# Softmax steps of VectorE taken in pairs, and three changes of sequence in the two layers, in a two-block transformer kernel

## The chip, the cores and the metric

The kernel runs on one core of one Trainium2 chip. The metric is the device time of one execution in microseconds (us). PE is TensorE, DVE is VectorE, ACT is ScalarE, POOL is GpSimd, SP is SyncE, which here only issues the transfers of weights.

## What is computed

256 tokens of width 1024 pass through two blocks, all in f32. Cut to what matters here:

```
# first block
h = rms_norm(x, g) * (1 + scale1) + shift1;  q, k, v, u, z = split(h @ w_in)      # 8 heads of 64
s = q @ k.T * 64**-0.5 + bias;  s = where(key <= query, s, -1e30);  p = softmax(s);  a = p @ v
mixed = (sigmoid(z1) * (a @ w_a) + sigmoid(z2) * (pool(u) @ w_p)) @ w_out;  x = x + gate1 * mixed
x = x + gate2 * moe(rms_norm(x) ...)       # 32 experts, the two best of a token
x = rms_norm(x, norm_f_g)
# second block, two layers
h = rms_norm(x);  a_q, a_i, a_zf, a_zb, a_g, b_u, c_q, c_k, c_v = split(h @ w_in)
o_a = hgrn2(a_q, a_i, a_zf, a_zb, a_g)     # gated scan, both directions
o_b = real(fft2(b_u))                      # over tokens and the channels of a group
o_c = attention(rotary(c_q), rotary(c_k), c_v)   # three dilated windows, here one softmax with a mask term, 8 heads
x = x + concat(o_a, o_b, o_c) @ w_out
x = x + square(relu(rms_norm(x) @ w_up)) @ w_down
```

## The kernel before

Every engine has a program of its own, written out in its final order (`pe_...`, `act_...`, `dve_...`). Nothing is rescheduled: an engine runs its list from top to bottom and stops at a semaphore until it is reached. PE writes into eight PSUM banks of 512 columns. `g.take` gives out the next bank of a rota and makes PE wait until the reader of the bank's previous content is done. `g.full` is the reader's wait for PE, and `g.evac` PE's wait for a reader. Weights come in tiles of 1 MB through a ring of SBUF slots that SP refills in the order of use.

**First block, attention.** `pe_first` does eight tiles of the gate projection (L541, two chunks `("gate", n)` each). After each tile comes a step of attention, `pe_attention_step(c)`: the scores of two heads (`pe_scores`, L566; two blocks of queries each, 128 keys for the first, 256 for the second), the turning of the probabilities of the step before (`pe_turn`, L575) and the product with v of the step before that (`pe_mix`, L589). DVE does for each of the four score tiles of a step in `dve_scores`: scale and add the bias (L1635), row maximum (L1638), wait for ACT's exponential with its row sum (ACT, L1272), reciprocal (L1640), multiplication (L1642). Between two steps DVE accumulates a product with the conditioning vector (`dve_ada`, L1650 and L1653) and later adds a bias to what PE makes of it (`dve_ada_bias`, L1661), which frees the PSUM bank of PE's L634. ACT does the exponentials, then copies the turned probabilities (L1279), then the gates (L1342), each time with a reload of its function table.

**The layers** (`pe_layer`, twice). PE alternates between projections (L541, L553) and the small products of the three mixers. `pe_hgrn` makes the far products (L1125, L1131) and seven levels of near ones (L1146); ACT copies the far products in `act_far` (L1566, L1567). `act_turn_halves` issues four transfers from ACT's queue (L1527), which swap the halves of c_q or c_k for the rotation. `pe_hgrn_out` (L1171, L1173) waits for ACT's last copies of the pair sums (L1456). Then come the first stage of the Fourier mixer (L989, four products), a product of ones (L993), and the attention in four steps of two heads. One step is S, scores (L1186); T, turning (L1199); M, the product with v (L1212). Between them lie four pieces O of the output projection, `pe_out_first` (L1231), which need none of the attention. In the text S1 is the scores of heads 2 and 3, S2 those of heads 4 and 5, S3 those of heads 6 and 7; T1, M1 and O1 likewise, and each counts from 0.

DVE's side of the layers' attention is a list in a fixed order:

```python
    for h in range(2, 8):
        dve_layer_score(e, g, l, h)
        if h > 2:
            dve_layer_prob(e, g, l, h - 1)
    dve_layer_prob(e, g, l, 7)
```

`dve_layer_score` reads the scores from PSUM (L2218) and takes the maximum (L2220); `dve_layer_prob` is the reciprocal (L2226) and two multiplications (L2230). T of a head waits in `pe_layer_turn` for that head's `dve_layer_prob`, by `e.wait_ge(g.s["prob_ready"], 8 * l + h + 1)`.

Of the kernel before, what the change touches and what calls it, by code (L numbers as in the profile page):

```python
# [8 lines left out]
AX = mybir.AxisListType  # L9

P = 128
D = 1024
S = 256
KC = D // P
ST = S // P
HEADS, DH = 8, 64
# [927 lines left out]
def pe_layer(e, g, l):  # L944
    s = g.s
    n = 2 + 2 * l
    ready = lambda k: h_ready(e, g, n, k)
    raw = lambda which: lambda k: e.wait_ge(s["xw"], KC * (2 * l + which) + k + 1)

    def project(tile, oc):  # L950
        w = g.filled(e, layer_tile(l, tile))
        for jj in range(2):
            pe_chunk(e, g, ("in", l, oc + jj), w, jj, 256, KC, g.h, ready)
        g.owed += 1

    def tokens(tile, j):
        w = g.filled(e, layer_tile(l, tile))
        pe_tokens(e, g, ("av", l, j), w, g.h, ready)
        g.owed += 1

    for tile in range(2):
        w = g.filled(e, layer_tile(l, tile))
        for jj in range(2):
            pe_chunk(e, g, ("in", l, 4 + 2 * tile + jj), w, jj, 256, KC, g.xw, raw(0))
            if tile == jj == 0 and l:
                pe_norm_added(e, g, n)
            if tile == 0 and jj == 1 and l == 0:
                pe_norm_two(e, g)
        g.owed += 1
    project(2, 0)  # L970
    tokens(3, 0)
    project(4, 10)
    project(5, 12)
    pe_hgrn(e, g, l, 0, 0)
    pe_hgrn(e, g, l, 0, 1)
    project(6, 14)
    project(7, 16)
    project(8, 2)
    pe_hgrn(e, g, l, 1, 0)
    project(9, 8)  # L980
    pe_hgrn(e, g, l, 1, 1)
    tokens(10, 1)
    pe_hgrn_out(e, g, l)
    for c in range(2):
        for tt in range(ST):
            u = g.take(e, ("V", l, c, tt))
            e.wait_ge(s["late_in"], 16)
            g.evac(e, "in", l, 8 + c)
            g.last(u, e.matmul(u.ap[:, 0:S], g.uT[:, c, tt * P:(tt + 1) * P], g.c("dft_c"), start=True, stop=True))  # L989
    u = g.take(e, ("os", l))  # L990
    e.wait_ge(s["o_square"], 2 * l + 2)
    for c in range(2):
        ins = e.matmul(u.ap[:, c * S:(c + 1) * S], g.c("headones"), g.tmp4[:, c, :], start=True, stop=True)  # L993
    g.last(u, ins)
    pe_layer_scores(e, g, l, 0)
    tokens(11, 2)
    for c in range(2):
        u = g.take(e, ("four", l, c))
        e.wait_ge(s["late_in"], 16)
        for tt in range(ST):  # L1000
            g.evac(e, "V", l, c, tt)
        for n4 in range(4):
            part, tt = n4 // 2, n4 % 2
            ins = e.matmul(u.ap[:, 0:S], g.V[:, tt, c, part * P:(part + 1) * P], g.c("dft_t", (part * ST + tt) * S, S), start=n4 == 0, stop=n4 == 3)
        g.last(u, ins)

    g.cycle, g.turn = range(4), 0
    out = []
    pe_layer_scores(e, g, l, 1)
    pe_layer_turn(e, g, l, 0)  # L1010
    pe_layer_scores(e, g, l, 2)
    pe_out_first(e, g, l, out)
    pe_layer_turn(e, g, l, 1)
    pe_layer_mix(e, g, l, 0)
    pe_layer_scores(e, g, l, 3)
    pe_out_first(e, g, l, out)
    pe_layer_turn(e, g, l, 2)
    pe_layer_mix(e, g, l, 1)
    pe_out_first(e, g, l, out)
    pe_layer_turn(e, g, l, 3)  # L1020
    pe_layer_mix(e, g, l, 2)
    pe_out_first(e, g, l, out)
    pe_layer_mix(e, g, l, 3)
    g.cycle, g.turn = range(8), 0
    for j in range(4):
        w = g.filled(e, layer_tile(l, 12 + j))
        for jj in range(2):
            for k in range(4, KC):
                g.evac(e, "m", l, k - 4)
                ins = e.matmul(out[j].ap[:, jj * S:(jj + 1) * S], w[:, k * 256 + jj * P:k * 256 + (jj + 1) * P], g.mix[:, k, :],  # L1030
                               start=False, stop=k == KC - 1, skip_group_check=True)
                if k < KC - 1:
                    g.hand_back(ins)
        g.last(out[j], ins)
        g.owed += 1

    for j in range(2):
        w = g.filled(e, layer_tile(l, 16 + j))
        for jj in range(2):
            oc = 2 * j + jj  # L1040
            pe_chunk(e, g, ("up", l, oc), w, jj, 256, KC, g.xw, raw(1))
            if oc == 0:
                pe_norm_added(e, g, n + 1)
        g.owed += 1
    for i in range(SEVENS):
        pe_seven(e, g, l, i)
    w = g.filled(e, layer_tile(l, 18 + SEVENS))
    e.wait_ge(s["hid_ready"], UPS * (l + 1))
    for jj in range(2):
        pe_chunk(e, g, ("down", l, jj), w, jj, 256, KC, g.hid[:, 24:32, :], lambda k: None)  # L1050
    g.owed += 1
# [102 lines left out]
def pe_hgrn_out(e, g, l):  # L1154
    for dr in range(2):
        for j in range(2):
            g.evac(e, "far", l, dr, j)
    e.wait_ge(g.s["far_out"], 4 * (l + 1))
    e.wait_ge(g.s["placed"], 2 * (l + 1))
    g.evac(e, "av", l, 0, 1)  # L1160
    for c in range(2):
        u = g.take(e, ("o", l, c))
        for tt in range(ST):
            for far in range(2):
                for j in range(2):
                    lo, hd = DH * j, 2 * c + j
                    v = slice(hd * DH, (hd + 1) * DH)
                    q = u.ap[lo:lo + DH, tt * P:(tt + 1) * P]
                    if far:
                        al = 4 * (1 - tt) + 2 * j + c  # L1170
                        ins = e.matmul(q, g.av[:, 1 - tt, v], g.AL[:, al * P:(al + 1) * P], start=False, stop=True)  # L1171
                    else:
                        ins = e.matmul(q, g.av[:, tt, v], g.AT[:, hd, tt * P:(tt + 1) * P], start=True, stop=False)  # L1173
                    if tt == far == 1 and j == 0:
                        ins.then_inc(g.s["o_half"], 1)
        g.last(u, ins)


def pe_layer_scores(e, g, l, c):

    us = [g.take(e, ("s", l, 2 * c + j)) for j in range(2)]
    e.wait_ge(g.s["rot_ready"], 4 * l + 3 + c // 2)
    for qt in range(ST):
        for j in range(2):
            lo = DH * j
            ins = e.matmul(us[j].ap[:, qt * S:(qt + 1) * S], g.cq[lo:lo + DH, c, qt * P:(qt + 1) * P], g.ck[lo:lo + DH, c, :],  # L1186
                           start=True, stop=True)
            if qt == 1:
                g.last(us[j], ins)


def pe_layer_turn(e, g, l, c):
    for j in range(2):
        h = 2 * c + j
        u = g.take(e, ("t", l, h))
        e.wait_ge(g.s["prob_ready"], 8 * l + h + 1)
        for kt in range(ST):
            for qt in range(ST):
                ins = e.transpose(u.ap[:, (2 * kt + qt) * P:(2 * kt + qt + 1) * P], g.prob[h % 4][:, qt * S + kt * P:qt * S + (kt + 1) * P],  # L1199
                                  g.c("ident"))  # L1200
        g.last(u, ins)
# [192 lines left out]
def act_layer(e, g, l):  # L1394
    s = g.s
# [40 lines left out]
            tokens(0)  # L1436
    for oc in range(10, 14):
        evict(oc)
    act_turn_halves(e, g, l, 0)
    act_far(e, g, l, 0)  # L1440
    for lv in range(NL):
        act_decay(e, g, l, 1, lv)
        if lv % 2 == 0:
# [15 lines left out]
    for c in range(2):  # L1459
        ps = g.full(e, "o", l, c)[:, 0:S]  # L1460
# [13 lines left out]
    for c in range(2):  # L1474
        ps = g.full(e, "four", l, c)[:, 0:S]
# [145 lines left out]


def dve_scores(e, g, A, c):
    for j in range(2):
        for qt in range(ST):
            s = 4 * c + 2 * j + qt
            nk, hd = A.keys(qt), 2 * c + j
            pr = A.pbuf[s % 8][:, 0:nk]
            m, total = g.small[:, 2 * s:2 * s + 1], g.small[:, 2 * s + 1:2 * s + 2]
            if s == 0:  # L1630
                A.first_score(e)
            if s >= 8:
                g.full(e, A.name, "t", c - 2, j)
            ps = g.full(e, A.name, "s", c, j, qt)
            g.read((A.name, "s", c, j, qt), e.scalar_tensor_tensor(out=pr, in0=ps[:, 0:nk], scalar=DH ** -0.5, in1=A.add(hd, qt),  # L1635
                                                                   op0=ALU.mult, op1=ALU.add))
            g.evac(e, A.name, "s", c, j, qt)
            e.tensor_reduce(m, pr, AX.X, ALU.max, negate=True).then_inc(g.s["row_max"], 1)  # L1638
            e.wait_ge(g.s["row_exp"], A.base + s + 1)
            g.step.up(e.reciprocal(total, total))  # L1640
            g.after(e)
            e.tensor_scalar(pr, pr, total, None, ALU.mult).then_inc(g.s["prob"], 1)  # L1642


def dve_ada(e, g, n):
# [809 lines left out]
```

## Time and profile before

| | |
|---|---|
| time, median of 3 runs | 1407.7 us (1407.31 to 1408.53) |
| time of the profiled execution | 1408.37 us |
| its span in the trace | 1406.6 us |
| mean granted clock of TensorE | 0.996 of full speed |
| PE busy | 1380.7 us, 98% |
| PE weight loads busy | 1061.7 us, 75% |
| DVE busy | 661.8 us, 47% |
| ACT busy | 264.2 us, 19% |
| POOL busy | 4.0 us |

The span is what the profiler sees; the time has 1.8 us more around it. The stages follow each other: first block without experts to about 235 us, experts to about 698 us, first layer to about 1047 us, second layer to the end. A busy PE includes the modelled end of each matmul, some 0.1 us after the next one has begun, so that a short pause between matmuls is a little longer than the idle time that the profile gives it.

### The profile page before, as it was taken

What the parts mean: (1) busy time and instruction counts of PE and PEld (TensorE: products, weight loads), DVE (VectorE), ACT (ScalarE), POOL (GpSimd) and SP (SyncE); (2) the same over time, 40 slices, a digit from 0 to 9 for tenths busy, and PEclk for the clock granted to TensorE, in tenths of its full rate; (3) what the DMA queues carried; (4) which work ended last, traced back from release to release, by engine and by line L of the source; (5) the groups of instructions that cost most, each with busy time, mean ns of one, the idle gap of its engine ahead of it and who ended that gap; (6) DMA issues with size and microseconds to landing.
All of it is one profiled execution on the core that took longest, in us unless ns stands there. A gap on an engine that the chain in (4) does not pass through costs nothing.

```text
span 1406.6 us, 22243 instructions
## 1 busy us (share of the span) xinstructions
PE 1380.7 (98%) x9402; PEld 1061.7 (75%) x9402; DVE 661.8 (47%) x1483; ACT 264.2 (19%) x565; POOL 4.0 (0%) x10
## 2 busy tenths in 40 slices
PE   9999999999999999999999999999999999999997
PEld 6888887454445544554488789999998878999997
DVE  2467554111111111111278837775445883777544
ACT  2234201100000000000243431220014343122000
POOL 0000000000000000000000000000000000000000
PEclk9999999999999999999999999999999999999999
DMA  9995656999999999999944224444544413444420
GB/s 392 354 398 197 265 215 274 422 422 420 420 420 422 420 421 420 423 421 421 418 166 132 83 101 171 178 161 169 181 150 150 151 61 124 171 158 179 165 76 31
DMA packets 51237, 362.95 MB, mean 258 GB/s; under 512 B 6064, under 2 KB 6384, under 8 KB 7872
## 3 DMA queue, kind: packets, MB, share of 16 engines
q1 hardware_dynamic: 48528, 353.39, 63.4%
q10 hardware_dynamic: 2032, 5.96, 1.4%
q0 software_dynamic: 576, 2.14, 0.4%
q8 instruction: 77, 1.26, 0.4%
q14 instruction: 24, 0.20, 0.0%
HBM read 358.31 MB, written 1.06 MB: 255 GB/s over the span
## 4 chain that ended last, share of the span: by engine, by line
PE 92%; DMA 2%; DVE 2%; ACT 1%; issue 1%; ACTq 0%; DVEq 0%; SPq 0%
PE bank L1094 26%; PE bank L839 22%; PE bank L541 19%; PE bank L553 4%; PE bank L827 4%; PE bank L849 4%; DMA ring<-in_weights 2%; PE bank L1231 2%; PE bank L658 2%; PE bank L1030 2%; PE bank L1186 1%; PE bank L1212 1%; PE bank L613 1%; PE bank L1146 1%; PE bank L1199 1%
## 5 line engine op out<-in xcount | busy, mean ns | idle before, releaser
L541 PE MATMUL bank<-h,ring 128*128 128x256 f32 x832 | 185.6, 383 | 0.8 <-issue 0.7
L541 PEld LDWEIGHTS bank<-h,ring 128*128 128x128 f32 x832 | 158.0, 191 | 23.8 <-issue 2.3
L839 PE MATMUL bank<-ring,x_s 128*64 128x512 f32 x768 | 167.8, 592 | 1.4 <-issue 0.9
L839 PEld LDWEIGHTS bank<-ring,x_s 128*64 128x64 f32 x768 | 56.1, 137 | 109.9 <-issue 109.9
L1094 PE MATMUL bank<-hid,ring 128*128 128x128 f32 x912 | 115.6, 275 | 0.0
L1094 PE MATMUL bank<-h,ring 128*128 128x128 f32 x896 | 113.8, 275 | 0.0
L1094 PEld LDWEIGHTS bank<-hid,ring 128*128 128x128 f32 x912 | 108.6, 192 | 0.0
L1094 PEld LDWEIGHTS bank<-h,ring 128*128 128x128 f32 x896 | 107.0, 192 | 0.1
L1936 DVE TENSOR_TENSOR act<-act,bank 128x512 f32<-128x512 f32 x16 | 11.0, 688 | 195.5 <-PE bank L839 195.5
L1094 PE MATMUL bank<-sq,ring 128*128 128x128 f32 x720 | 95.1, 275 | 0.0
L1094 PEld LDWEIGHTS bank<-sq,ring 128*128 128x128 f32 x720 | 87.6, 192 | 0.0
L839 PE MATMUL bank<-ring,a_s 128*64 128x512 f32 x384 | 85.0, 595 | 0.0
L553 PE MATMUL bank<-ring,h 128*128 128x256 f32 x320 | 71.2, 381 | 0.0
L1094 PE MATMUL bank<-ring 128*128 128x128 f32 x512 | 67.6, 275 | 0.0
L553 PEld LDWEIGHTS bank<-ring,h 128*128 128x128 f32 x320 | 60.2, 190 | 9.3 <-issue 1.3
L1919 DVE TENSOR_TENSOR x_s<-bank,mod 128x512 f32<-128x512 f32 x32 | 22.1, 692 | 95.7 <-PE bank L827 95.7
L839 PEld LDWEIGHTS bank<-ring,a_s 128*64 128x64 f32 x384 | 26.5, 137 | 49.4 <-issue 48.0
L1094 PEld LDWEIGHTS bank<-ring 128*128 128x128 f32 x512 | 62.3, 192 | 0.0
L849 PEld LDWEIGHTS bank<-put,gy 128*128 128x128 f32 x256 | 47.3, 190 | 19.8 <-issue 14.0
L827 PE MATMUL bank<-pick,h 128*128 128x128 f32 x512 | 61.4, 279 | 0.7 <-DVE pick L1911 0.7
L827 PEld LDWEIGHTS bank<-pick,h 128*128 128x128 f32 x512 | 59.9, 196 | 0.8 <-issue 0.8
L849 PE MATMUL bank<-put,gy 128*128 128x256 f32 x256 | 59.5, 385 | 1.0 <-DVE gy L1943 1.0
(353 smaller groups left out, 1734.7 us busy)
## 6 DMA issues: line engine op xcount, KB each, us to landing
ring<-in_weights SPq DMA_DIRECT2D x288, 1024.0 KB, 12.4
ringx<-in_weights SPq DMA_DIRECT2D x48, 1024.0 KB, 19.6
x<-in_x SPq DMA_DIRECT2D x1, 1024.0 KB, 5.1
pool_a<-in_cst ACTq DMA_DIRECT2D x1, 1024.0 KB, 6.2
bias<-bias_rows POOLq DMA_DIRECT2D x1, 1024.0 KB, 16.9
ring<-cq ACTq DMA_DIRECT2D x8, 128.0 KB
ring<-ck ACTq DMA_DIRECT2D x8, 128.0 KB, 2.4
out<-h ACTq DMA_DIRECT2D x2, 512.0 KB, 3.6
```

The lines of the kernel that those rows point to most:

```text
L541: ins = e.matmul(u.ap[:, 0:S], w[:, k * width + j * P:k * width + (j + 1) * P], acts[:, k, :], start=k == 0, stop=k == kc - 1)
L553: ins = e.matmul(u.ap[:, 0:256], acts[:, k, tt * P:(tt + 1) * P], w[:, k * 256:(k + 1) * 256], start=k == 0, stop=k == KC - 1)
L613: ins = e.matmul(u.ap[32 * q:32 * q + 32, 0:256], g.spread[:, k, :], w[:, k * 256:(k + 1) * 256], start=m == 0, stop=m == 1)
L658: ins = e.matmul(u.ap[:, 0:S], w[:, k * 256 + jj * P:k * 256 + (jj + 1) * P], g.h[:, k, :], start=k == 0, stop=k == KC - 1)
L827: ins = e.matmul(g.bank[bank + k // 4][:, (k % 4) * P:(k % 4 + 1) * P], g.h_tok[:, tt, k * P:(k + 1) * P], g.pick[:, tt * P:(tt + 1) * P], ...
L839: ins = e.matmul(g.bank[bank][ex * SLOTS:(ex + 1) * SLOTS, :], stat(m)[:, ex * SLOTS:(ex + 1) * SLOTS], pair[ex][:, m * 512:(m + 1) * 512] ...
L849: ins = e.matmul(g.bank[4 + oc // 2][:, (oc % 2) * S:(oc % 2 + 1) * S], gy[:, oc * P:(oc + 1) * P], put[:, :], start=p == oc % 2 == 0, sto ...
L1030: ins = e.matmul(out[j].ap[:, jj * S:(jj + 1) * S], w[:, k * 256 + jj * P:k * 256 + (jj + 1) * P], g.mix[:, k, :], start=False, stop=k == ...
L1094: ins = e.matmul(u.ap[:, at * P:(at + 1) * P], a[:, k, :], act[:, k, :], start=k == 0 and (of == 1 or (b == 0 and first)), stop=k == 3 and ...
L1146: ins = e.matmul(us[j].ap[HB * b:HB * b + HB, lv * HB:(lv + 1) * HB], k, q, start=True, stop=True)
L1231: e.matmul(u.ap[:, jj * S:(jj + 1) * S], w[:, k * 256 + jj * P:k * 256 + (jj + 1) * P], g.mix[:, k, :], start=k == jj == 0, stop=False, sk ...
L1919: e.tensor_tensor(g.x_s[:, 512 * half:512 * half + 512].rearrange("p (k t) -> p k t", k=4), g.bank[bank + half][:, :].rearrange("p (k t) - ...
```

## The change

Four edits, none of which adds or removes an instruction.

1. `dve_scores` is split into `dve_one_score` (scale, add, maximum) and `dve_one_prob` (wait for the exponential, reciprocal, multiplication). The score of tile n+1 now comes ahead of the division of tile n.
2. In `pe_layer` the first half of the Fourier mixer's first stage stands ahead of `pe_hgrn_out`, the second behind it.
3. In `pe_layer` each of the pieces O0, O1 and O2 moves ahead of the scores that it followed.
4. In `act_layer` the copies of `act_far` stand ahead of the four transfers of `act_turn_halves`.

```diff
@@ pe_layer
     tokens(10, 1)
+    pe_channels(e, g, l, 0)
     pe_hgrn_out(e, g, l)
-    for c in range(2):
-        for tt in range(ST):
-            u = g.take(e, ("V", l, c, tt))
-            e.wait_ge(s["late_in"], 16)
-            g.evac(e, "in", l, 8 + c)
-            g.last(u, e.matmul(u.ap[:, 0:S], g.uT[:, c, tt * P:(tt + 1) * P], g.c("dft_c"), start=True, stop=True))
+    pe_channels(e, g, l, 1)
...
     pe_layer_scores(e, g, l, 1)
     pe_layer_turn(e, g, l, 0)
+    pe_out_first(e, g, l, out)
     pe_layer_scores(e, g, l, 2)
-    pe_out_first(e, g, l, out)
     pe_layer_turn(e, g, l, 1)
     pe_layer_mix(e, g, l, 0)
+    pe_out_first(e, g, l, out)
     pe_layer_scores(e, g, l, 3)
-    pe_out_first(e, g, l, out)
     pe_layer_turn(e, g, l, 2)
     pe_layer_mix(e, g, l, 1)
     pe_out_first(e, g, l, out)
@@ act_layer
+    act_far(e, g, l, 0)
     act_turn_halves(e, g, l, 0)
-    act_far(e, g, l, 0)
@@ dve_scores
+    for n in range(5):
+        if n < 4:
+            dve_one_score(e, g, A, c, n)
+        if n:
+            dve_one_prob(e, g, A, 4 * c + n - 1)
```

`pe_channels(e, g, l, c)` is the removed loop's body for one c, and `dve_one_score` and `dve_one_prob` are the two halves of the old loop's body, with the same waits and semaphores.

On DVE, in the first step of the first block's attention (`p1_0` to `p1_3` are the four score tiles), the program of before reads:

```order
L1635 SCALAR_TENSOR_TENSOR p1_0_56<-bank4,bias_49 128x128
L1638 TENSOR_REDUCE small<-p1_0_56 128x1
L1640 RECIPROCAL small<-small 128x1
L1642 TENSOR_SCALAR p1_0_56<-p1_0_56,small 128x128
L1635 SCALAR_TENSOR_TENSOR p1_1_57<-bank6,bias_49 128x256
L1638 TENSOR_REDUCE small<-p1_1_57 128x1
L1640 RECIPROCAL small<-small 128x1
L1642 TENSOR_SCALAR p1_1_57<-p1_1_57,small 128x256
```

and that of the change:

```order
L1647 SCALAR_TENSOR_TENSOR p1_0_56<-bank4,bias_49 128x128
L1650 TENSOR_REDUCE small<-p1_0_56 128x1
L1647 SCALAR_TENSOR_TENSOR p1_1_57<-bank6,bias_49 128x256
L1650 TENSOR_REDUCE small<-p1_1_57 128x1
L1656 RECIPROCAL small<-small 128x1
L1658 TENSOR_SCALAR p1_0_56<-p1_0_56,small 128x128
L1647 SCALAR_TENSOR_TENSOR p1_2_58<-bank5,bias_49 128x128
L1650 TENSOR_REDUCE small<-p1_2_58 128x1
L1656 RECIPROCAL small<-small 128x1
L1658 TENSOR_SCALAR p1_1_57<-p1_1_57,small 128x256
```

Each reciprocal now has the next tile's two instructions ahead of it; only the last of a step, of `p1_3`, has none.

On PE, in the attention of a layer, the program of before reads (L1004 is the end of the Fourier mixer, L1186 is S, L1199 T, L1231 O, L1212 M):

```order
L1004 MATMUL bank<-cst,cum 128x256 x8
L1186 MATMUL bank<-ck,cq 128x256 x4
L1199 MATMUL bank<-cst,hm 128x128 x8
L1186 MATMUL bank<-ck,cq 128x256 x4
L1231 MATMUL bank<-mixed,ring 128x256 x8
L1199 MATMUL bank<-cst,hm 128x128 x8
L1212 MATMUL bank<-hm,cv 64x256 x4
L1186 MATMUL bank<-ck,cq 128x256 x4
L1231 MATMUL bank<-mixed,ring 128x256 x8
L1199 MATMUL bank<-cst,hm 128x128 x8
```

and that of the change (L1191 is S, L1204 T, L1236 O, L1217 M):

```order
L1000 MATMUL bank<-cst,cum 128x256 x8
L1191 MATMUL bank<-ck,cq 128x256 x4
L1204 MATMUL bank<-cst,hm 128x128 x8
L1236 MATMUL bank<-mixed,ring 128x256 x8
L1191 MATMUL bank<-ck,cq 128x256 x4
L1204 MATMUL bank<-cst,hm 128x128 x8
L1217 MATMUL bank<-hm,cv 64x256 x4
L1236 MATMUL bank<-mixed,ring 128x256 x8
L1191 MATMUL bank<-ck,cq 128x256 x4
L1204 MATMUL bank<-cst,hm 128x128 x8
```

O stood between S2 and T1 and between S3 and T2; it now stands ahead of S2 and of S3, and T follows S at once.

DVE's program in that stretch is the same in both kernels. From the score of head 2 it reads:

```order
L2218 SCALAR_TENSOR_TENSOR hm_120<-bank0,cst 128x512
L2220 TENSOR_REDUCE small<-hm_120 128x2
L2218 SCALAR_TENSOR_TENSOR hm_120<-bank1,cst 128x512
L2220 TENSOR_REDUCE small<-hm_120 128x2
L2226 RECIPROCAL small<-small 128x2
L2230 TENSOR_SCALAR hm_120<-hm_120,small 128x256 x2
L2218 SCALAR_TENSOR_TENSOR hm_120<-bank0,cst 128x512
L2220 TENSOR_REDUCE small<-hm_120 128x2
L2226 RECIPROCAL small<-small 128x2
L2230 TENSOR_SCALAR hm_120<-hm_120,small 128x256 x2
```

These are score 2, score 3, division 2, score 4 and division 3: the division of head 3 stands behind the score of head 4. Nothing moved here.

## Rows read from the trace of the kernel before

**Rows 1.** The page, chain that ended last: shares by engine.

```profile
PE 92%; DMA 2%; DVE 2%; ACT 1%; issue 1%; ACTq 0%; DVEq 0%; SPq 0%
```

**Rows 2.** Waits of PE: total us, times, longest us.

```profile
PE bank L1186 <- issue: 2.2, 2, 1.1
PE bank L1146 <- ACT sq L1567: 1.4, 2, 0.7
PE bank L1173 <- ACT sq L1456: 1.3, 2, 0.6
...
PE bank L839 <- DMA ring<-in_weights: 0.5, 1, 0.5
```

**Rows 3.** Timeline of PE, first block: start us, us, instruction, [idle before].

```profile
101.26 0.92 PE L566 MATMUL bank<-k,q 64*128 64x128 f32 x6
102.88 0.70 PE L566 MATMUL bank<-k,q 64*128 64x256 f32 x2 [0.70 <-ACT pt L1279]
...
105.04 0.55 PE L575 MATMUL bank<-cst,p 128*128 128x128 f32 x3 [0.99 <-ACT gate L1342]
...
107.12 8.83 PE L541 MATMUL bank<-h,ring 128*128 128x256 f32 x32 [0.73 <-issue]
...
116.22 0.93 PE L566 MATMUL bank<-k,q 64*128 64x128 f32 x8
...
118.69 7.17 PE L541 MATMUL bank<-h,ring 128*128 128x256 f32 x32
```

**Rows 4.** Timeline of DVE, first block.

```profile
91.84 0.35 DVE L1650 TENSOR_SCALAR ada_acc<-ring,cact 128x256 f32<-128x256 f32 x1
...
106.87 0.15 DVE L1661 TENSOR_TENSOR mod<-bank,prm 128x2 f32<-128x2 f32 x1
```

**Rows 5.** Waits of DVE from 84 to 126 us: total, times, longest.

```profile
DVE small L1640 <- ACT p L1272: 9.8, 16, 0.7
```

**Rows 6.** Windows: length, busy us of PE, PEld, DVE, ACT, POOL; granted clock, DMA share, GB/s.

```profile
101.26:107.12 5.86, 3.44 (x23) 1.95 (x23) 4.88 (x14) 4.75 (x8) 0.00 (x0) 1.00 0.89 323
107.12:110.60 3.48, 3.48 (x9) 2.76 (x10) 2.11 (x9) 1.09 (x4) 0.00 (x0) 0.52 0.22 87
803.56:807.90 4.34, 3.22 (x25) 2.30 (x24) 3.07 (x7) 3.16 (x7) 0.00 (x0) 1.00 0.00 0
...
240.00:245.00 5.00, 4.94 (x24) 2.12 (x26) 1.39 (x8) 0.00 (x0) 0.00 (x0) 1.00 0.08 10
```

**Rows 7.** Waits of PE's weight loads: total, times, longest.

```profile
PEld bank L1125 <- DVE hm L2278: 0.3, 1, 0.3
```

**Rows 8.** Timeline of DVE, second layer, end of the second decay.

```profile
1115.39 0.42 DVE L2278 TENSOR_TENSOR hm<-mixed,kk 128x256 f32<-128x256 f32 x1
```

**Rows 9.** Timeline of PE, second layer, first product after it.

```profile
1116.72 0.71 PE L1125 MATMUL bank<-hm 64*128 64x128 f32 x8
```

**Rows 10.** Timeline of DVE, first layer, third addition of the rotation.

```profile
790.90 0.69 DVE L2074 TENSOR_TENSOR ck<-ck,ring 128x512 f32<-128x512 f32 x1
```

**Rows 11.** Timeline of PE, first layer, attention.

```profile
791.93 1.13 PE L1186 MATMUL bank<-ck,cq 64*128 64x256 f32 x8
...
803.56 1.13 PE L1186 MATMUL bank<-ck,cq 64*128 64x256 f32 x8
...
806.84 1.13 PE L1186 MATMUL bank<-ck,cq 64*128 64x256 f32 x8 [1.12 <-issue]
807.90 3.72 PE L1231 MATMUL bank<-mixed,ring 128*128 128x256 f32 x16
811.46 1.04 PE L1199 MATMUL bank<-cst,hm 128*128 128x128 f32 x8
```

**Rows 12.** Timeline of DVE, first layer, attention.

```profile
804.73 0.69 DVE L2218 SCALAR_TENSOR_TENSOR hm<-bank,cst 128x512 f32<-128x512 f32 x1 [1.78 <-PE bank L1186]
...
807.37 0.15 DVE L2226 RECIPROCAL small<-small 128x2 f32<-128x2 f32 x1
807.56 0.62 DVE L2230 TENSOR_SCALAR hm<-hm,small 128x256 f32<-128x256 f32 x2
```

More of the change, by code:

```diff
@@ L1176, in pe_hgrn_out, with pe_channels @@
         g.last(u, ins)
+def pe_channels(e, g, l, c):
+    for tt in range(ST):
+        u = g.take(e, ("V", l, c, tt))
+        e.wait_ge(g.s["late_in"], 16)
+        g.evac(e, "in", l, 8 + c)
+        g.last(u, e.matmul(u.ap[:, 0:S], g.uT[:, c, tt * P:(tt + 1) * P], g.c("dft_c"), start=True, stop=True))
 def pe_layer_scores(e, g, l, c):
@@ L1623, in dve_scores, with dve_one_score, dve_one_prob @@
 def dve_scores(e, g, A, c):
[L1624 to L1642, printed above, removed]
+    for n in range(5):
[3 more added lines that the diff above has]
+            dve_one_prob(e, g, A, 4 * c + n - 1)
+def dve_one_score(e, g, A, c, n):
+    j, qt, s = n // 2, n % 2, 4 * c + n
+    nk, hd = A.keys(qt), 2 * c + j
+    pr = A.pbuf[s % 8][:, 0:nk]
+    if s == 0:
+        A.first_score(e)
+    if s >= 8:
+        g.full(e, A.name, "t", c - 2, j)
+    ps = g.full(e, A.name, "s", c, j, qt)
+    g.read((A.name, "s", c, j, qt), e.scalar_tensor_tensor(out=pr, in0=ps[:, 0:nk], scalar=DH ** -0.5, in1=A.add(hd, qt),
+                                                           op0=ALU.mult, op1=ALU.add))
+    g.evac(e, A.name, "s", c, j, qt)
+    e.tensor_reduce(g.small[:, 2 * s:2 * s + 1], pr, AX.X, ALU.max, negate=True).then_inc(g.s["row_max"], 1)
+def dve_one_prob(e, g, A, s):
+    pr, total = A.pbuf[s % 8][:, 0:A.keys(s % 2)], g.small[:, 2 * s + 1:2 * s + 2]
+    e.wait_ge(g.s["row_exp"], A.base + s + 1)
+    g.step.up(e.reciprocal(total, total))
+    g.after(e)
+    e.tensor_scalar(pr, pr, total, None, ALU.mult).then_inc(g.s["prob"], 1)
 def dve_ada(e, g, n):
```

## The prediction

> **What bounds the kernel now.** I read the chain that ended last first: 92% of it is PE [rows 1]. So only what shortens PE's list counts, and that means pauses and slow stretches, since no edit removes an instruction. Next I read the waits of PE [rows 2]. They are few and short; the first three come twice because there are two layers. Two of these (L1146 for `act_far`, L1173 for the last copies of the pair sums) are those at which edits 4 and 2 aim, and L1186 is S2, at which edit 3 aims. The largest loss doesn't show in that table. It is in the first block's third attention step, so I went to PE's timeline there [rows 3], to DVE's [rows 4, 5], and to the windows for the clock [rows 6].
>
> **Edit 1, the first block.** The third step begins at 101.26 and its next projection at 107.12, 5.86 us. The fourth step has the same products and takes 118.69 - 116.22 = 2.47 us [rows 3]. The difference, 3.39 us, is three pauses: for ACT's copies of the turned tiles, for the gate, and one called "issue". The last is a bank: PE waits for DVE's L1661 at 106.87, which ends at 107.02 [rows 4]. All three are late for one reason. ACT and DVE run one after another on each score tile, and DVE waits 9.8 us in 16 tiles for ACT's exponential [rows 5], 2.45 us a step. A round of DVE is then longer than a round of PE, which is why PE catches up by the third step.
>
> With the next score ahead of the division, the wait is covered: a score of the next tile is 0.5 to 0.9 us of DVE and the wait 0.7 at most. Only the last tile of a step has less in front of it (the division of the one before). I take 2.4 of 2.45 us a step as gone. The product that now starts at 91.84 [rows 4] starts near 89.4, and L1661, two steps' savings earlier, near 102.0. PE wants that bank only at 101.26 + 2.47 = 103.73. ACT's exponentials of the second step end some 4 us sooner, so its copies and gates, too, are ready before PE asks. All 3.39 us should go.
>
> Behind the pauses, the projection at 107.12 takes 8.83 us where the same 32 matmuls at 118.69 take 7.17 [rows 3]. The granted clock shows why: 0.52 of full speed in that stretch, thus nearly all of it at 1.2 instead of 2.4 GHz, after a stretch in which PE was busy 3.44 of 5.86 us [rows 6]. Without the pauses I expect no fall: another 1.66 us. Edit 1: -5.05 us, with bounds of -3.39 (a fall comes anyway) and -5.05. The saving is passed on. The experts' weights are limited by transfer near their end, but PE's only wait for it is 0.5 us [rows 2], and at 240 to 245 the transfers stand almost still (DMA share 0.08) until PE frees slots [rows 6]. So they start earlier by what PE gains.
>
> **Edit 4, ACT's copies ahead of four transfers.** It takes 0.7 us off PE in each layer [rows 2]. In the first layer PE then meets DVE: the weight load of L1125 already waits 0.3 us for DVE's L2278 [rows 7], and DVE's list up to there doesn't depend on the copies. Worth 0 (at most 0.7). In the second layer DVE is done at 1115.81 and PE arrives at 1116.72 [rows 8, 9], a slack of 0.9: worth 0.7. The transfers that now go later feed the rotation, some 40 us on; cover enough.
>
> **Edit 2, half of the Fourier stage ahead of `pe_hgrn_out`.** The four products fill the 0.6 us pause of L1173 [rows 2]. But S0 needs DVE's third addition, which ends at 790.90 + 0.69 = 791.59 [rows 10], and S0 starts at 791.93 [rows 11]. About 0.1 us lies between a semaphore and PE's start, so 0.25 us a layer is the gain (0 to 0.34), and the rest turns into a wait at S0.
>
> **Edit 3, O ahead of S.** It fills the pause of 1.12 us before S2 [rows 11]; O (3.56 us, 811.46 - 807.90) needs nothing late. But it takes away what stood between S2 and T1, and what T1 needs is made from S2's result in DVE's fixed order: score 4, then division 3. Without score 4 division 3 isn't reached, though its own data have long been there. From the start of S to DVE's start on it: 804.73 - 803.56 = 1.17 us. One score until the next instruction: (807.37 - 804.73) / 2 = 1.32. One division until its end: 807.56 + 0.62 - 807.37 = 0.81 [rows 11, 12]. PE's start after it, 0.1. Sum 3.40 us from S2's start to the second half of T1. PE now gets there after S (807.90 - 806.84 = 1.06) and half of T (1.04 / 2), 1.58 us. It waits 1.8 us. Before, T1 began 4.62 us behind S2, and the chain was hidden by O.
>
> The same happens at S3 and T2, by division 5 behind score 6; T3 has no scores ahead of it. Queued behind the waiting T are M, O and the next S, so all of the rest moves. Each layer: two waits of 1.8 less the pause of 1.1, +2.5 us. Both: +5.0. Bounds for one such wait: 1.4 (if DVE gets S's first head 0.4 earlier) to 2.0.
>
> The sum before the clock: -5.05 - 0.7 - 0.5 + 5.0 = -1.25 us.
>
> **The clock.** The new waits stand amid short products. Once in these rows a like stretch was followed by 1.2 GHz: busy 3.44 of 5.86 us, for a loss of 1.66 us. The stretch around S2, busy 3.22 of 4.34 us, kept 2.4 GHz [rows 6]. S, T and M take some 1 us each, so from S2 through T1 and M0 the changed kernel would be busy about 3.0 of 4.9 us, 62%. That is nearer to the stretch that lost the clock (59%) than to the one that kept it (74%). There are four such places, each worth 0 to 1.66 us. I take two or three of them, 2.5 x 1.66 = +4.15. Total +2.9 us: 1411.3 against the profiled 1408.37, and against the median of 1407.7, 1410.6 us.
>
> The Trainium skill ("TensorE: Matmul & The Clock Gate", "Why this matters for your kernels") warns only of idle gaps longer than any here. By that rule none of the four waits would cost clock and the sum would be 1406.4. The trace speaks against it: the three pauses of the third step are 0.70, 0.99 and 0.73 us [rows 3], and the clock fell.
>
> **The rivals.**
> - Two or three falls, as above: 1409.8 to 1411.4 us. Chance 0.45.
> - All four fall: -1.25 + 6.6 = +5.4, 1413.1 us. For it speaks that the four places are alike. 0.17.
> - None or one falls: 1406.4 to 1408.1 us. A single pause of 1.8 us in 4.9 may not be like three in 5.9, and O, long and dense, follows soon. 0.27.
> - The other side, faster. T1 and T2 don't wait, because division 3 is ready before them. Then edit 3 gains its 1.1 us a layer: -5.05 - 0.7 - 0.5 - 2.2 = -8.45, 1399.2 us. It would need the chain from S to T to be at most 1.6 instead of 3.4 us; its four terms are measured, so this is small, 0.05. Even then three falls of the clock somewhere would be needed to undo it.
> - Edit 1 doesn't do what it says: PE still waits in the third step, by ACT's table loads or by a weight tile for DVE, or the experts' transfers swallow the gain. Then the -5.05 is 0 and the rest stands: 1407.7 + 3.8 = 1411.5 us with no fall, 1415.6 with two or three. Against it: the slack of 1.7 us at the bank and the idle transfers. 0.06.
>
> **How the numbers follow.** 0.2% is 2.8 us, about what a measurement here can tell from no change, so the borders are 1404.9 and 1410.5. The likeliest case has its middle at 1410.6, its own range is 1408.8 to 1412.4, and the border cuts it nearly in half. Same: 0.22 of it and 0.25 of the one with fewer falls, 0.47 less what its low end may give, 0.45. Slower: 0.23 + 0.17 + 0.06 and a rest, 0.47. Faster: 0.05 and 0.03 from the low end of no falls with a 1 us better sum, 0.08. The range leaves out the far rivals: from one microsecond under the case without a fall's middle, 1406.0, to a little over all four, 1413.8.
>
> **What would show it.** In the first block: the third step 2.5 us long, no wait of L566 and L575, clock 1.00 behind it, DVE's waits of 9.8 us nearly gone. In the layers: no wait at S2, but T with a wait of 1.6 to 2.0 us for DVE's multiplication twice a layer, four in all; L1173's wait gone and a short one at S0; L1125 of the first layer where DVE lets it. Windows behind each T wait show 0.5 or 1.00: this decides between the cases. Wrong would be a T that starts right behind S, a first block still pausing, or a second layer whose L1125 doesn't come 0.7 us earlier.

## The result, and the profile after

The changed kernel takes 1414.95 us (median of 6 runs, 1413.6 to 1416.34), that of before 1408.05 us (6 runs, 1407.21 to 1408.53). The ratio is 1.005 with a 95% interval of 1.0038 to 1.0063: slower by 5.4 to 8.9 us, where 1410.6 us was forecast, in a range that ended at 1413.8. The traced execution of the changed kernel took 1413.78 us, at the low end of its runs.

The waits of PE in the changed kernel (total us, times, longest):

```profile
PE bank L1204 <- DVE hm L2246: 7.2, 4, 1.8
PE bank L1142 <- issue: 3.3, 2, 2.0
...
PE bank L1191 <- DVE ck L2090: 0.4, 2, 0.2
```

Against [rows 2] the reader sees three things. The pause of S2 is gone, and T (L1204) has four waits of 1.8 us for DVE's multiplication in its place. The wait of the near products for ACT is gone, and a longer pause with no named releaser has come. The wait of L1173 is gone, and one of 0.2 us at S0 (L1191) has come in its place.

PE's timeline in the third step of the first block's attention answers to [rows 3]:

```profile
101.19 0.93 PE L566 MATMUL bank<-k,q 64*128 64x128 f32 x8
102.05 0.88 PE L575 MATMUL bank<-cst,p 128*128 128x128 f32 x6
102.86 0.87 PE L589 MATMUL bank<-pt,v 128*64 128x256 f32 x8
103.66 7.17 PE L541 MATMUL bank<-h,ring 128*128 128x256 f32 x32
...
113.56 7.17 PE L541 MATMUL bank<-h,ring 128*128 128x256 f32 x32
```

The step takes 2.47 us and the projection behind it 7.17 instead of 8.83. The row that stood at 118.69 stands at 113.56, 5.13 us earlier. DVE's waits for ACT's exponential in the same stretch, where [rows 5] had 9.8 us in 16 waits:

```profile
DVE small L1656 <- ACT p L1277: 1.1, 4, 0.3
```

PE's timeline of the first layer's attention in the changed kernel, for [rows 11]:

```profile
797.40 1.13 PE L1191 MATMUL bank<-ck,cq 64*128 64x256 f32 x8
798.47 1.09 PE L1204 MATMUL bank<-cst,hm 128*128 128x128 f32 x8
799.40 3.62 PE L1236 MATMUL bank<-mixed,ring 128*128 128x256 f32 x16
802.95 1.13 PE L1191 MATMUL bank<-ck,cq 64*128 64x256 f32 x8
804.01 0.66 PE L1204 MATMUL bank<-cst,hm 128*128 128x128 f32 x4
806.46 0.70 PE L1204 MATMUL bank<-cst,hm 128*128 128x128 f32 x4 [1.79 <-DVE hm L2246]
807.09 1.98 PE L1217 MATMUL bank<-hm,cv 128*64 128x256 f32 x8
809.00 4.34 PE L1236 MATMUL bank<-mixed,ring 128*128 128x256 f32 x16
...
816.79 0.79 PE L1204 MATMUL bank<-cst,hm 128*128 128x128 f32 x4 [1.79 <-DVE hm L2246]
817.50 1.98 PE L1217 MATMUL bank<-hm,cv 128*64 128x256 f32 x8
819.41 4.26 PE L1236 MATMUL bank<-mixed,ring 128*128 128x256 f32 x16
...
824.47 1.08 PE L1217 MATMUL bank<-hm,cv 128*64 128x256 f32 x8
825.48 3.72 PE L1236 MATMUL bank<-mixed,ring 128*128 128x256 f32 x16
```

S2 starts at 802.95 with no pause. The first half of T1 runs, the second waits 1.79 us. Behind each wait the products are slow: M takes 1.98 us and O 4.34 and 4.26, where the M and the O behind T3, which doesn't wait, take 1.08 and 3.72. DVE's timeline at the first of the waits:

```profile
804.18 0.69 DVE L2234 SCALAR_TENSOR_TENSOR hm<-bank,cst 128x512 f32<-128x512 f32 x1 [2.16 <-PE bank L1191]
804.91 0.69 DVE L2236 TENSOR_REDUCE small<-hm 128x2 f32<-128x512 f32 x1
805.51 0.15 DVE L2242 RECIPROCAL small<-small 128x2 f32<-128x2 f32 x1
805.70 0.62 DVE L2246 TENSOR_SCALAR hm<-hm,small 128x256 f32<-128x256 f32 x2
```

DVE itself stands idle for 2.16 us until S2 delivers. Then it does score 4, and only behind it division 3, which ends at 806.32; T1's second half starts at 806.46. That is 3.51 us behind the start of S2, where the forecast had worked out 3.40.

The clock in windows of the changed kernel (length, busy us by engine, granted clock, DMA share, GB/s):

```profile
807.00:810.80 3.80, 3.80 (x14) 2.33 (x14) 1.32 (x4) 2.32 (x7) 0.00 (x0) 0.57 0.00 0
...
817.30:820.70 3.40, 3.40 (x14) 1.85 (x13) 2.13 (x7) 2.32 (x7) 0.00 (x0) 0.52 0.04 7
...
103.66:110.60 6.94, 6.94 (x34) 6.14 (x33) 6.24 (x19) 4.17 (x11) 0.00 (x0) 1.00 0.63 256
```

Behind both waits the clock is at 1.2 GHz for most of the window. In the second layer it is the same: 0.59 from 1162.0 to 1166.0 and 0.51 from 1172.2 to 1175.6. Behind the first block's third step it stays at 2.4 GHz.

Where the time went, by the start of the same product in both traces. S1 of the first layer starts 6.16 us earlier than before (797.40 against 803.56). Of this lead 5.13 us is edit 1's, and 1.5 us is a fall of the clock in the routing of the experts that of these two traces only that of before has (last section); some 0.5 us is given back on the way. By the end of that attention the lead is gone: the first product behind it starts at 830.15, before at 830.25. So the stretch from S1 to that product takes 32.75 us instead of 26.69, 6.06 us more. The second layer repeats it: 1152.39 to 1185.14, before 1152.63 to 1179.31, 32.75 instead of 26.68 us.

### The profile page after: what moved, and what is told of

The parts are those of the page before. It is cut to its first block, busy times and chain, and to the rows that moved or that the text cites. A ratio compares the mean times of both kernels' runs of the same rounds, so it can differ in the third digit from the quotient of the medians.

```text
span 1412.0 us, 22243 instructions
## 1 busy us (share of the span) xinstructions
PE 1383.7 (98%) x9402; PEld 1060.8 (75%) x9402; DVE 661.2 (47%) x1483; ACT 264.2 (19%) x565; POOL 4.0 (0%) x10
## 4 chain that ended last, share of the span: by engine, by line
PE 93%; DVE 3%; DMA 2%; issue 1%; ACT 0%; DVEq 0%; SPq 0%; ACTq 0%
PE bank L1090 26%; PE bank L839 22%; PE bank L541 20%; PE bank L553 4%; PE bank L849 4%; PE bank L827 4%; DMA ring<-in_weights 2%; PE bank L1236 2%; PE bank L658 2%; PE bank L1026 2%; PE bank L1142 1%; PE bank L1217 1%; PE bank L1191 1%; PE bank L613 1%; PE bank L1000 0%
## 5 line engine op out<-in xcount | busy, mean ns | idle before, releaser
L827 PE MATMUL bank<-pick,h 128*128 128x128 f32 x512 | 59.9, 275 | 0.7 <-DVE pick L1927 0.7
L827 PEld LDWEIGHTS bank<-pick,h 128*128 128x128 f32 x512 | 58.4, 192 | 0.8 <-issue 0.8
```

The lines of the kernel that those rows point to most:

```text
L827: ins = e.matmul(g.bank[bank + k // 4][:, (k % 4) * P:(k % 4 + 1) * P], g.h_tok[:, tt, k * P:(k + 1) * P], g.pick[:, tt * P:(tt + 1) * P], ...
```

## The experiments

Times with a ratio below stand beside the kernel before on the same chip (median there 1408.6 to 1409.1 us). Differences in us are (ratio - 1) x 1409. In the kernel before PE's and DVE's lines have the numbers of the sections above.

**One edit at a time.** `e1_pairs` is the kernel before with the new `dve_scores`, `e2_out_early` the one with O0 and O1 moved ahead of S2 and S3, `e3_far_first` the one with `act_far` first. Those two pieces are all that edit 3 moves: O2 stands behind M1 in both kernels, though the list of the edits names it as well. Edit 2 has no run by itself.

```diff
# e2_out_early
     pe_layer_turn(e, g, l, 0)
+    pe_out_first(e, g, l, out)
     pe_layer_scores(e, g, l, 2)
-    pe_out_first(e, g, l, out)
...
+    pe_out_first(e, g, l, out)
     pe_layer_scores(e, g, l, 3)
-    pe_out_first(e, g, l, out)
# e3_far_first
+    act_far(e, g, l, 0)
     act_turn_halves(e, g, l, 0)
-    act_far(e, g, l, 0)
```

> Edit 1 alone. Theory: the third step's pauses (3.4 us) and the slow stretch behind them (1.66 us) go, -5.1 us, about 1402.9. Rival: the gain of the first block is taken back by the experts' transfers, then under 2 us of it are left.

Measured: 1403.94 us, ratio 0.9964 (0.9951 to 0.9978), -5.1 us: the theory's size. The experts' transfers take back little of it: in this trace the lead over before is 5.0 us where the experts' first product starts and 4.2 us where the first layer's products for the scan begin, so 0.8 us at most.

> Edit 3 alone. Theory: per layer two waits of T of 1.8 us, less the pause of 1.1 us at S2, and two falls of the clock of 1.66 us: +5.8 us a layer, +11.7 us in all, about 1419.5. Rival, waits without the clock: +5 us. Second rival, that the loss is another edit's: under +3 us.

Measured: 1421.48 us, ratio 1.0085 (1.0072 to 1.0099), +12.0 us. This is the theory with the clock; for the waits alone the forecast had +5. Its trace has the same four waits as the changed kernel, and slow windows behind them:

```profile
PE bank L1199 <- DVE hm L2230: 7.2, 4, 1.8
```

```profile
813.00:817.60 4.60, 3.88 (x16) 2.34 (x17) 2.54 (x7) 3.30 (x11) 0.00 (x0) 0.65 0.00 0
824.30:828.00 3.70, 3.70 (x15) 2.13 (x14) 2.41 (x8) 2.37 (x8) 0.00 (x0) 0.54 0.03 7
```

The first fence is its waits of PE, the second its windows in the first layer, clock 0.65 and 0.54.

> Edit 4 alone. Theory that PE is held in the near products by the supply of its instructions: the wait for ACT turns into a pause with no releaser that ends at the same time, 0 us (within 0.5). The forecast's step said -0.7 us in the second layer.

Measured: 1408.85 us, ratio 1.0 (0.9991 to 1.0009): nothing. The waits of PE's near products in its trace, and then in `e10_no_far` (below), which keeps the old order in ACT:

```profile
PE bank L1146 <- issue: 2.9, 2, 1.9
```

```profile
PE bank L1142 <- ACT sq L1572: 1.4, 2, 0.7
```

The wait for ACT is gone with the edit, and a pause with no releaser stands in its place.

**The waits, with PE kept busy in them.** In `e4_fill` and `e4b_fill4` the changed kernel gets products of ones into a bank that is free then, eight and four in each of the four waits.

```diff
@@ pe_layer_turn (c is the pair of heads, j the head in it)
         u = g.take(e, ("t", l, h))
+        if c in (1, 2) and j == 1:
+            g.idle(e, 7)
+            for i in range(8):        # 4 in e4b_fill4
+                e.matmul(g.bank[7][:, 0:S], g.c("ones"), g.c("dft_c"), start=True, stop=True)
         e.wait_ge(g.s["prob_ready"], 8 * l + h + 1)
```

> The changed kernel with eight products of ones, written to a bank that nobody reads, in each of the four waits of T (1.7 us of PE's work where it would stand still). Theory that the clock falls because PE is idle amid short products: no stretch at half clock in the layers, T no later than before, 4 x 1.66 = 6.6 us faster than the changed kernel, about 1408.3. Rival, that the falls have another cause (the turning, or a load on the engine): the same as the changed kernel, 1415 or later.

Measured: 1414.67 us, ratio 1.0038 (1.0024 to 1.0052), as slow as the changed kernel. The expected time was missed, and the time alone would have spoken for the rival. The eight products take 3.5 us and not 1.7: T's second half starts 5.02 us behind S2, where it was 3.51 in the changed kernel. That is 1.5 us more, four times, nearly what the four falls cost. But no window in the layers' attention has a low clock, which speaks for the theory. With the filling cut to the length of the wait:

> As e4_fill, with four products of ones instead of eight in each wait, since eight took 3.5 us where the wait was 1.8. Theory that idle time amid short products makes the clock fall: no half clock in the layers and T no later than in the changed kernel, so the four falls are saved whole, some 6 us faster than the changed kernel, within 1.5 us of before. Rival: falls as in the changed kernel, +6 us on before.

Measured: 1409.62 us, ratio 1.0003 (0.9994 to 1.0012), thus 6.6 us less than the changed kernel's 1.005. PE's timeline and two windows of this kernel:

```profile
806.47 0.66 PE L1208 MATMUL bank<-cst,hm 128*128 128x128 f32 x4
806.97 1.89 PE L1204 MATMUL bank<-cst 128*128 128x256 f32 x8
808.84 0.66 PE L1208 MATMUL bank<-cst,hm 128*128 128x128 f32 x4
809.42 1.08 PE L1221 MATMUL bank<-hm,cv 128*64 128x256 f32 x8
810.44 3.72 PE L1240 MATMUL bank<-mixed,ring 128*128 128x256 f32 x16
```

```profile
803.00:813.00 10.00, 10.00 (x56) 7.54 (x55) 5.45 (x15) 6.03 (x20) 0.00 (x0) 1.00 0.00 0
813.00:823.00 10.00, 10.00 (x57) 7.52 (x56) 4.82 (x13) 3.41 (x11) 0.00 (x0) 1.00 0.01 2
```

The row at 806.97 is the filling; the profile counts each of its four f32 products twice. T is as late as ever, 2.37 us behind its first half (in the changed kernel 2.45), since nothing was done about DVE. But M takes 1.08 and O 3.72 us, and the clock is 1.00. Useless work in the waits saves what the falls cost, 6.6 us for four. The two ratios come from separate measurements and leave 3.7 to 9.7 us for that saving. The traces say it more closely: from S1 to the product behind the attention this kernel takes 29.46 us in the first layer, the changed one 32.75, thus 3.29 us less, and as much in the second. This is shown, not argued.

**Without edit 3, and with DVE's order mended.** `e5_no_out` is the changed kernel with edit 3 undone. `e6_div_first` keeps all four edits and turns DVE's list:

```diff
-    for h in range(2, 8):
-        dve_layer_score(e, g, l, h)
-        if h > 2:
-            dve_layer_prob(e, g, l, h - 1)
-    dve_layer_prob(e, g, l, 7)
+    for h in range(2, 8, 2):
+        dve_layer_score(e, g, l, h)
+        dve_layer_score(e, g, l, h + 1)
+        dve_layer_prob(e, g, l, h)
+        dve_layer_prob(e, g, l, h + 1)
```

> The changed kernel without edit 3 (O back behind S). Theory: what is left is edit 1's 5.1 us and edit 2's 0.5, edit 4 gives nothing: 5.6 us faster than before. Rival, by the forecast's step on edit 4: 6.3 us faster.

Measured: 1402.64 us, ratio 0.9958 (0.9944 to 0.9971), -5.9 us; the interval holds both expectations.

> The changed kernel, with DVE's list in the layers turned so that both divisions of a pair of heads stand ahead of the next pair's scores. Theory that T waits because division 3 stands behind score 4: no wait at T, no fall in the layers, and no pause at S2: 7.8 us faster than before, 14 us faster than the changed kernel. Rival, that T waits for the time that the exponential and the division take by themselves: a wait of T stays, with slow stretches.

Measured: 1402.32 us, ratio 0.9957 (0.9943 to 0.997), -6.1 us, with an interval (-8.0 to -4.2) that just holds the 7.8 expected, and no better than `e5_no_out` by these runs. The trace is as expected:

```profile
803.65 1.13 PE L1191 MATMUL bank<-ck,cq 64*128 64x256 f32 x8
804.72 1.10 PE L1204 MATMUL bank<-cst,hm 128*128 128x128 f32 x8
805.74 1.08 PE L1217 MATMUL bank<-hm,cv 128*64 128x256 f32 x8
806.76 3.72 PE L1236 MATMUL bank<-mixed,ring 128*128 128x256 f32 x16
```

T runs in one piece behind S. So the two kernels ran again on one chip, with a third that leaves edit 4 out:

> The kernel of e6_div_first once more, beside that of e5_no_out on one chip. Theory: the pause at S2 (1.1 us a layer) is filled, so 2.2 us faster than the kernel with O behind S. Rival, that the gain is lost again behind the attention: no difference.

> The kernel of e5_no_out once more on the chip of e9_div_again: 5.6 us faster than before, 2.2 us slower than e9_div_again.

Measured: 1401.71 us, ratio 0.9947 (0.9935 to 0.996), -7.5 us; and 1404.56 us, ratio 0.9966 (0.9954 to 0.9978), -4.8 us. The medians are 2.85 us apart, near the 2.2 expected, though the intervals overlap a little. Over both pairs of runs the mended order gains 0.3 and 2.85 us, so the times alone leave the size open. The traces settle it for the attention, as the table below shows: 25.60 us in either layer instead of 26.69, which makes 2.2 us for both.

> The kernel of e6_div_first without edit 4. Theory that the supply of instructions holds PE either way: same as e9_div_again within 0.7 us. Rival, by the forecast's step on edit 4: 0.7 us slower.

Measured: 1401.34 us, ratio 0.9944 (0.9931 to 0.9957): no slower without edit 4. This is the fastest kernel of the study, though `e9_div_again` can't be told from it.

**The same stretch in all traces.** The length from S1's start to the start of the first product behind the attention varies by under 0.1 us between layers and executions of one order. That makes it a closer measure of edit 3 than the times, and the causes can be read one by one:

| order of O and of DVE's list | first layer, us | second layer, us |
|---|---|---|
| O behind S (kernel before; `e1_pairs`, `e3_far_first`, `e5_no_out`, `e7_halves_late` and `e11_no_out_again` within 0.01) | 26.69 | 26.68 |
| O ahead of S, changed kernel | 32.75 | 32.75 |
| O ahead of S, nothing else changed (`e2_out_early`) | 32.81 | 32.84 |
| O ahead of S, changed kernel with the waits overfilled (`e4_fill`) | 32.51 | 32.52 |
| O ahead of S, changed kernel with the waits filled (`e4b_fill4`) | 29.46 | 29.45 |
| O ahead of S, DVE's divisions first (`e6_div_first`, `e9_div_again`, `e10_no_far`) | 25.60 | 25.60 |

The waits cost 29.46 - 26.69 = 2.77 us a layer, the two falls 32.75 - 29.46 = 3.29, and with DVE's list mended edit 3 gains 1.09.

**The pause in the near products.** `e7_halves_late` is the kernel before with `act_far` first and the four transfers behind the second exponential of the second decay (`if lv == 1: act_turn_halves(e, g, l, 0)`). `e8_spread` is `e6_div_first` with a projection between the two groups:

```diff
+    project(6, 14)
     pe_hgrn(e, g, l, 0, 1)
-    project(6, 14)
```

> The kernel before with edit 4, and the four transfers of the halves of q put behind the second exponential of the second decay, some 12 us later. Theory that the pause in the near products is the supply of instructions alone: it stays as it is with edit 4, near 1.3 and 2.0 us, time as before within 0.5 us. Rival, that these transfers hold up the loading of instructions: the pause shrinks to under half, and the second layer's products after it come up to 1.5 us earlier.

Measured: 1409.7 us, ratio 1.0004 (0.9995 to 1.0014). The pauses are 1.02 and 0.97 us; in `e3_far_first` they are 1.91 and 0.94, in the changed kernel 1.29 and 1.99. They aren't gone, and they vary by a microsecond between kernels with the same sequence there, so one trace can't say whether the transfers have a part in it. The pause can also bring a fall of its own. Nine traces have edit 4 and the two groups back to back, eighteen pauses of 0.9 to 2.1 us in all. Behind sixteen of them the clock stays, behind two it falls, both in the second layer: 0.50 from 1096.61 to 1100.00 in `e4_fill`, 0.50 from 1091.62 to 1095.00 in `e11_no_out_again`.

> As e6_div_first, with a projection (7 us) moved in between the two groups of near products of the first direction. Theory that PE runs out of instructions in a long row of 64-column products: with the row cut in two the pause with no releaser goes to under 0.5 us in both layers. DVE's second half of pairs starts up to 1 us later, so the time is within 1.5 us of e6_div_first. Rival, that the pause belongs to the place and not to the row's length: it stays at 1 to 2 us in one of the two groups.

Measured: 1408.24 us, ratio 0.9995 (0.9986 to 1.0004), 6.5 us slower than the same kernel without the projection on the same chip (`e9_div_again`, 1401.71): the expectation on the time was wrong. Its waits of PE:

```profile
PE bank L1121 <- DVE hm L2294: 7.1, 2, 3.5
PE bank L613 <- DMA ring<-in_weights: 1.0, 1, 1.0
```

The near products (L1142) have no pause any more, in either group of either layer, as the theory on the length of the row says. The price is another: DVE now idles until the second group comes, is late with its decay, and PE stands 3.5 us before L1121 in each layer, with slow windows behind it. Its windows of one microsecond show clock 0.50 from 764 to 770 us. That the pause is a supply of instructions remains argued. Shown, by this one arrangement, is that it goes when the two groups no longer stand back to back.

## Why the prediction was wrong

By its own steps:

- **Edit 1**, -5.05: right. 5.13 us in the trace, -5.1 us alone (3.1 to 6.9). The three pauses and the fall went together, and DVE's waits fell from 9.8 to 1.1 us.
- **Passed on through the experts**: right but for a little. PE's wait for a tile there is 0.9 instead of 0.5 us, so 0.4 us is given back.
- **Edit 2**, -0.25 a layer: right. A wait of 0.2 us for the rotation has taken the place of the 0.6 us one at L1173. From the last near product to S0 PE takes 12.45 us in the nine traces with the edit and 12.63 in the five without, -0.19 a layer.
- **Edit 3's waits**, +2.5 a layer: right, if a little small. Four waits of 1.8 us, sum 7.2, by the chain from S to score 4 to division 3. `e6_div_first` takes the chain apart, and the waits go. By the table they cost 2.77 a layer.
- **Edit 4**, -0.7 us in the second layer: wrong. The step took the 0.7 us wait for ACT as time that PE would gain. PE would have stopped there anyway: the second layer of the kernel before has, in the same row of products and behind that wait, another pause with no releaser. It is this row of its timeline, which the forecast hadn't looked at:

```profile
1095.37 0.39 PE L1146 MATMUL bank<-hm 64*64 64x64 f32 x10 [1.03 <-issue]
```

In the changed kernel PE goes on from there at 1095.32, 6.36 us after the group's first product, before at 1095.37, 6.31 us after it. `e3_far_first` and `e10_no_far` both give nothing for the edit. Why PE pauses there is open.

- **The clock**, +4.15 for "two or three of them": the term that failed. All four fell, in each trace that has the waits (the changed kernel, `e2_out_early`), and none in the attention where the waits are filled or gone. Four cost 6.6 us in the pair `e4b_fill4` and changed kernel, 1.65 each; the size per fall was right, the count was not. The forecast's own comparison had the new stretches nearer to the one that lost the clock, and all four alike. It was softened to 2.5 by the thought that one pause differs from three, for which no row spoke. The rule of the Trainium skill ("TensorE: Matmul & The Clock Gate", "Why this matters for your kernels"), which warns only of longer idle gaps, is not enough here: PE kept to it and the clock fell all the same, behind waits of 1.8 us, in four places of four in both traces that have them.

Put together with these corrections: -5.1 + 0.4 for edit 1 and what the experts give back, -0.4 for edit 2, 0 for edit 4, +5.5 for the waits, +6.6 for the falls. That is +7.0 us. The medians are 6.9 us apart, and the ratio says +5.4 to +8.9. The case "all four fall" stood at 1413.1 us with 17%; it was the right case, too low by edit 4's 0.7, by 0.5 for the waits and by 0.4 for the experts, and the range ended a microsecond too soon.

## What to carry to other kernels

Before moving filler work ahead of a producer, look at what it stood in front of: work that fills a short pause may be the cover of a longer chain, and an in-order engine adds to that chain whatever its list has in between. The mending was on the other engine, where two divisions ahead of the next scores made the same sequence on PE free. And where rows of the same kernel show the clock falling behind such pauses, count a wait of PE amid short products at its length plus what the clock loses behind it, here 1.8 + 1.65 us, and count it for every place that is alike.

## What the runs showed of the hardware

- A fall of the clock cost nearly as much as the wait ahead of it (1.65 us behind 1.8), and products that nobody reads avoid it: 6.6 us of 1415 for four.
- The fall isn't bound to the attention, and the same stretch can fall in one execution and not in another. In the kernel before the windows from 233.81 to 237.00 us, behind two waits of the routing, have clock 0.51; in the changed kernel the same products run at 1.00:

```profile
233.81:237.00 3.19, 3.19 (x15) 3.19 (x16) 2.15 (x12) 0.00 (x0) 0.00 (x0) 0.51 1.01 424
```

```profile
228.69:232.30 3.61, 3.61 (x32) 3.61 (x32) 2.85 (x13) 0.00 (x0) 0.00 (x0) 1.00 1.02 429
```

  The sequence and the waits there are the same in both. It is so within one kernel too: the 32 products L827 take 3.81 us in `e6_div_first` and 5.44 in `e9_div_again`, behind a wait of 0.74 us in both, and these two are the same kernel on two chips. Seven of the fourteen traces have this fall. So about 1.5 us comes and goes from one execution to the next. It is likely a part of the spread of 3 us among runs of one kernel.
- PE stops for 0.9 to 2.1 us, with no releaser, near the end of some 200 products of 64 columns in 3 us, in both layers of all nine traces that have them back to back and ACT's copies early (edit 4). In the four traces with the old order of ACT it waits 0.7 us for ACT in that row and then stops for 0.4 to 1.0 us, or, in one layer of the kernel before and one of `e10_no_far`, not at all.
